# Two experts with 96 places share a group of 128 columns with two experts of 32 places: 25 groups instead of 26 in each mixture-of-experts layer

## The chip, the core and the metric

One core of a Trainium2 chip runs the whole kernel as one program. The metric is the device time of one execution in microseconds; all figures below are in us unless marked ns. The engines are called PE (TensorE, the matmuls), PEld (its weight loads), DVE (VectorE), ACT (ScalarE), POOL (GpSimd) and SP (SyncE, which issues the large DMAs).

## What is computed

A trunk of two layers over one sequence of 256 tokens with 1024 channels, all in fp32: a forgetting-attention layer and a native-sparse-attention layer, each followed by a mixture of experts. The mixture is what matters here:

```python
scores = jax.nn.sigmoid(h @ w_router)                 # 256 tokens x 64 experts
_, top_e = lax.top_k(scores + b_router, TOP_K)        # 8 experts of each token
top_s = jnp.take_along_axis(scores, top_e, axis=-1)
top_w = top_s / jnp.sum(top_s, axis=-1, keepdims=True) * ROUTED_SCALE
...
y = (jax.nn.silu(xb @ w_eg[e]) * (xb @ w_eu[e])) @ w_ed[e]     # 1024 -> 256 -> 1024
routed = segment_sum(y * row_w[:, None], row_tok, num_segments=T)
```

Every expert has 3 MB of weights (gate, up and down); 64 experts in each of two layers are 384 MB, which are read once.

## The kernel before, in words

**The ring of weights.** All large weights pass through `ring`, 14 slots of 1 MB. SP issues one DMA for each unit of 1 MB in the order of `ring_order` (L89): a unit may be issued once the unit 14 places before it has been used. For the experts, `used_by` (L1246) says what that is: the first halves of gate and up of a group are free at its semaphore `gu_half_out`, the second halves at `gu_out`, the down weights at the second `y_out`. An expert has three units, two of gate and up (`gate_up_unit`, L357) and one of down (`down_unit`, L360). After the last expert of the first layer the ring goes on with the units of the key/value projection, the adaLN vectors and the compression of the second layer.

**The groups.** PE works on experts in groups that together fill 128 columns, one column for each place, a place being one token of one expert. Experts 0 to 3 are static and take ranks 0 to 3; the other 60 are ranked at run time by how many tokens they have, most first. `expert_groups` (L63) fixes how many places a rank has: ranks 0 to 3 have 64 places and form two pairs, ranks 4 to 7 have 128 each and are alone (`LONE`), ranks 8 to 31 have 64 and form 12 pairs (`PAIRED`), ranks 32 to 63 have 32 and form 8 quads (`QUADS`). That makes 26 groups, in this order: two static pairs; four times a quad and a lone expert; four times three pairs and a quad. `GROUPS` is that list. If an expert has more tokens than places, a loop after the groups (`more_items`, L851) treats the rest in passes of 64 places. `capacity` (L1338, on POOL at the very start) holds the places of each rank, from which the number of such passes is worked out.

**A group on PE** (`pe_moe`, the loop at L951) is, in this order:
1. Gate and up, `pe_gate_up` (L817, matmul L823): for each of 8 blocks of 128 channels one matmul of 512 moving columns for each expert of the group, whose stationary operand is that expert's slice of the gathered tokens, 128, 64 or 32 columns wide. Each writes its own partitions of one PSUM bank. Four blocks come from the first half of the units, four from the second.
2. The gather of the next group's tokens, `pe_gather` (L813), by a one-hot matrix that DVE has made (`hot`, L1085): 16 matmuls.
3. Two transposes of the weighted one-hot matrix (L839) and two of the hidden rows (L841).
4. The combine of the group before, `pe_combine` (L846): 4 matmuls of 512 columns.
5. Down, `pe_down` (L831): 2 halves of 512 channels times 2 blocks of 128 hidden columns, for each expert one matmul of 512 columns.

Each fp32 matmul of the code is two load-and-matmul instructions in the trace, so a block of a lone expert shows x2, of a pair x4, of a quad x8.

ACT works on the silu (L1038), the copies of the gathered tokens (L1030) and of the transposes (L1043); DVE on the product (L1147), the one-hot matrices (L1087, L1095) and the scaling of the output (L1154). The instructions of one group are spread so that PE has work between the two halves of each of these chains. In the last group there is no gather, so step 5 comes sooner.

Of the kernel before, what the change touches and what calls it, by code (L numbers as in the profile page):

```python
# [24 lines left out]
ALU = mybir.AluOpType  # L25
# [3 lines left out]
P = 128  # L29
D = 1024  # L30
SEQ = 256
NT = SEQ // P
KC = D // P
# [18 lines left out]
PASS = 64  # L52
# [2 lines left out]


STATIC = 4
LONE = range(STATIC, 8)
PAIRED = range(8, 32)
QUADS = range(32, 64)  # L60


def expert_groups():  # L63

    lone = [[r] for r in LONE]
    pairs = [[r, r + 1] for r in PAIRED[::2]]
    quads = [list(range(r, r + 4)) for r in QUADS[::4]]
    out = [[0, 1], [2, 3]]
    for i in range(4):
        out += [quads[i], lone[i]]  # L70
    for i in range(4):
        out += pairs[3 * i:3 * i + 3] + [quads[4 + i]]
    return out


GROUPS = expert_groups()


# [68 lines left out]
def build(nc, a, out):  # L147
    with ExitStack() as ctx:
# [11 lines left out]
        PS = ctx.enter_context(nc.psum_tensor("PS", [P, 8, 512], F32))  # L160
        ring = sb("ring", [P, SLOTS, UNIT])
# [15 lines left out]
        iota = sb("iota", [P, IOTA])  # L177
# [24 lines left out]
        slot_ranked, weight_ranked = ranked[:, 0], ranked[:, 1]  # L202
        capacity = sb("capacity", [N_EXP, 1])
# [77 lines left out]
        x_more = cut(4864, [KC, PASS])  # L281
# [93 lines left out]
        group_sem = {n: sem(n) for n in PER_GROUP}  # L375
# [412 lines left out]
        GATHER, GU, Y0 = 4, 5, 6  # L788
# [69 lines left out]
        def pe_moe(pe_, layer):  # L858
            m = moe_sem[layer]
# [63 lines left out]
            for kind in range(2):  # L923
                for t in range(NT):
                    c = (kind * NT + t) * N_EXP
# [23 lines left out]
                return mm  # L949

            for g, group in enumerate(GROUPS):  # L951
                w = P // len(group)
                last = g == len(GROUPS) - 1
                pe_.wait_ge(*by_group("x_ready", layer, 2 * g + 2))
                for half in range(2):
                    for i in range(len(group)):
                        landed(pe_, gate_up_unit(layer, g, i, half))
                    slots = [slot_no(gate_up_unit(layer, g, i, half)) for i in range(len(group))]
                    pe_gate_up(pe_, slots, x_pair[g % 2], w, half
                               ).then_inc(group_sem["gu_out" if half else "gu_half_out"], 1)  # L960
                if g == 0:
                    item_ends()
# [22 lines left out]
                    landed(pe_, down_unit(layer, g, i))  # L985
                downs = [slot_no(down_unit(layer, g, i)) for i in range(len(group))]
                for half in range(2):
                    pe_down(pe_, downs, hidT[g % 2], w, half).then_inc(group_sem["y_out"], 1)
            combine(len(GROUPS) - 1).then_inc(unit_done, 3 * N_EXP)

            def one_more(i):
                pe_.wait_ge(*of_item(m, "onehot", i))
                pe_gather(pe_, hot_more, range(KC)).then_inc(m["more_products"], 1)
                pe_.wait_ge(*of_item(m, "x", i))
                pe_.wait_ge(m["more_loaded"], i * 48 + 48)
                pe_gate_up(pe_, [0], x_more, PASS, 0)
                pe_gate_up(pe_, [1], x_more, PASS, 1).then_inc(m["more_products"], 1)
# [4 lines left out]
                pe_down(pe_, [2], hidT[0], PASS, 0)  # L1002
                pe_down(pe_, [2], hidT[0], PASS, 1).then_inc(m["more_products"], 1)
# [53 lines left out]
        def dve_moe(done, layer):  # L1057
# [24 lines left out]
            def group_shape(x, n):  # L1082
                return x.to_broadcast([P, NT, n, P // n])

            def hot(g, slots):  # L1085
                n = len(GROUPS[g])
                return dve.tensor_tensor(one_hot[g % 2].rearrange("p t (n s) -> p t n s", n=n),  # L1087
                                         group_shape(iota[:, 1:1 + P // n].unsqueeze(1).unsqueeze(1), n),
                                         group_shape(slots[:, :, GROUPS[g][0]:GROUPS[g][0] + n].unsqueeze(3), n),
                                         ALU.is_equal)  # L1090

            def hot_weighted(g):
                n = len(GROUPS[g])
                r = GROUPS[g][0]
                return dve.tensor_tensor(hot_w.rearrange("p t (n s) -> p t n s", n=n),  # L1095
                                         one_hot[g % 2].rearrange("p t (n s) -> p t n s", n=n),
                                         group_shape(weight_ranked[:, :, r:r + n].unsqueeze(3), n), ALU.mult)
# [167 lines left out]
        def _(pool):  # L1265
# [67 lines left out]
            for e in range(STATIC):  # L1333
# [1 line left out]
                                        base=-e, pattern=[[1, N_EXP]], channel_multiplier=0))  # L1335
                done(pool.affine_select(out=key_col[:, :], in_=key_col[:, :], compare_op=ALU.not_equal, fill=FRONT * (STATIC - e),
                                        base=-e, pattern=[[0, 1]], channel_multiplier=1))
            done(pool.memset(capacity[:, :], float(P)))  # L1338
            for base, sign, slots in ((LONE.stop - 1, -1, 64), (-LONE.start, 1, 64), (QUADS.start - 1, -1, 32)):
                done(pool.affine_select(out=capacity[:, :], in_=capacity[:, :], compare_op=ALU.is_ge, fill=float(slots),  # L1340
                                        base=base, pattern=[[0, 1]], channel_multiplier=sign))
# [658 lines left out]
```

## Time and profile before

| | us |
|---|---|
| median of 3 runs | 1584.86 (1583.45 to 1586.05) |
| the profiled execution, its own time | 1586.27 |
| its span, first to last instruction | 1584.4 |
| PE busy | 1480.9 (93% of the span) |
| experts of layer 0, first gate/up to last combine | 304 to 776 |
| experts of layer 1 | 1106 to 1578 |

The profile comes from one execution. A timeline row gives the start, the duration, the engine, the line and the operation, then `out<-in`, the stationary shape (`128*32` is 128 rows by 32 columns) with the moving shape, and how many instructions the row merges. `[0.81 <-issue]` is the engine's idle time before it; "issue" is time in which the engine waited for nothing that the profile shows. For a DMA the answer on its line gives the number of issues, and the time from the issue to the landing. A stretch's row gives the busy time of each engine in it, the TensorE clock that was granted as a share of full speed, the mean busy share of the 16 DMA engines and what they moved in GB/s.

### The profile page before, as it was taken

To read this page: it belongs to the slowest core of one execution; us is meant where nothing else is said; L and a number is where in the kernel's file an instruction comes from. 1 tells how busy PE (TensorE), PEld (TensorE's weight loads), DVE (VectorE), ACT (ScalarE), POOL (GpSimd) and SP (SyncE) were. 2 spreads that over 40 slices of the span, in tenths; PEclk is the share of its full clock that TensorE was granted. 3 is DMA by queue.
4 is the path that set the end of the run, shared out by engine and by line. 5 is a ranking of instruction groups with operands and counts; after the bars stand their busy time and mean duration, and the time that the engine had idled before them with its cause. 6 is when DMAs were issued, how large, how long until landed. Compare 5 with 4: busy or idle time off the path is not lost.

```text
span 1584.4 us, 21198 instructions
## 1 busy us (share of the span) xinstructions
PE 1480.9 (93%) x8561; PEld 888.8 (56%) x8561; DVE 417.6 (26%) x969; ACT 280.8 (18%) x549; POOL 31.4 (2%) x81
## 2 busy tenths in 40 slices
PE   4999988999999999999798868789999999999998
PEld 2777777644555444454376757676455454544443
DVE  0466432111111111111367247522111111111111
ACT  2211332111111111111212215421111111111110
POOL 4000001000000000000000000001000000000000
PEclk9999987999999999999999768889999999999999
DMA  9967602399999999999999810031999999999996
GB/s 342 413 265 309 255 27 87 135 376 422 421 421 422 374 421 420 421 420 422 417 404 384 360 53 1 1 113 34 368 421 422 421 420 375 422 420 421 420 421 264
DMA packets 71315, 512.38 MB, mean 323 GB/s; under 512 B 8176, under 2 KB 8400, under 8 KB 9264
## 3 DMA queue, kind: packets, MB, share of 16 engines
q1 hardware_dynamic: 69984, 508.59, 78.5%
q0 software_dynamic: 800, 1.28, 0.4%
q8 instruction: 69, 1.13, 0.3%
q10 hardware_dynamic: 432, 1.13, 0.2%
q14 instruction: 30, 0.25, 0.0%
HBM read 509.92 MB, written 1.05 MB: 322 GB/s over the span
## 4 chain that ended last, share of the span: by engine, by line
PE 87%; DVE 5%; ACT 3%; issue 2%; DMA 1%; DVEq 0%; ACTq 0%
PE PS L823 23%; PE PS L446 13%; PE PS L813 12%; PE PS L831 12%; PE PS L846 11%; PE PS L875 2%; PE PS L616 2%; PE PS L404 2%; PE PS L469 2%; PE PS L483 1%; DMA h<-in_x 1%; PE PS L913 1%; PE PS L867 1%; DVE acc L527 1%; PE PS L586 1%
## 5 line engine op out<-in xcount | busy, mean ns | idle before, releaser
L823 PE MATMUL PS<-ring,scratch 128*32 128x512 f32 (+2 forms) x2048 | 367.8, 594 | 1.4 <-ACT scratch L1030 1.4
L823 PEld LDWEIGHTS PS<-ring,scratch 128*32 128x32 f32 (+2 forms) x2048 | 118.8, 127 | 243.7 <-issue 241.9
L446 PE MATMUL PS<-ring,uT 128*128 128x256 f32 x960 | 224.3, 395 | 2.9 <-ACT uT L417 1.8
L813 PEld LDWEIGHTS PS<-scratch,u 128*128 128x128 f32 x1664 | 190.8, 192 | 39.5 <-issue 37.6
L446 PEld LDWEIGHTS PS<-ring,uT 128*128 128x128 f32 x960 | 189.2, 199 | 31.8 <-ACT uT L417 2.6
L813 PE MATMUL PS<-scratch,u 128*128 128x128 f32 x1664 | 199.6, 278 | 1.4 <-ACT scratch L1030 1.4
L1154 DVE TENSOR_TENSOR scratch<-PS,gate_row 128x512 f32<-128x512 f32 x104 | 72.0, 692 | 464.1 <-PE PS L831 464.1
L831 PE MATMUL PS<-ring,scratch 128*32 128x512 f32 (+2 forms) x1024 | 189.3, 596 | 1.2 <-DVE item_first_i L1139 1.2
L846 PE MATMUL PS<-scratch 128*128 128x512 f32 x416 | 187.3, 593 | 0.0
L1038 ACT ACTIVATE scratch<-PS 128x256 f32<-128x256 f32 x52 | 20.0, 384 | 675.7 <-PE PS L823 675.7
L831 PEld LDWEIGHTS PS<-ring,scratch 128*32 128x32 f32 (+2 forms) x1024 | 56.8, 126 | 125.5 <-issue 123.8
L846 PEld LDWEIGHTS PS<-scratch 128*128 128x128 f32 x416 | 75.0, 190 | 76.3 <-issue 74.6
L1147 DVE TENSOR_TENSOR scratch<-scratch,PS 128x256 f32<-128x256 f32 x52 | 21.9, 422 | 337.5 <-ACT scratch L1038 337.5
L1030 ACT ACTIVATE scratch<-PS 128x512 f32<-128x512 f32 x104 | 62.1, 597 | 162.9 <-PE PS L813 162.9
L527 DVE SCALAR_TENSOR_TENSOR acc<-ring,cond,acc 128x256 f32<-128x256 f32 x168 | 81.5, 485 | 6.0
L483 PE MATMUL PS<-ring,scratch 128*32 128x256 f32 x512 | 42.5, 460 | 12.2 <-DVE scratch L1687 6.8
L616 PE MATMUL PS<-scratch,uT 128*128 128x65 f32 x288 | 38.4, 284 | 12.2 <-ACT uT L639 12.2
L616 PEld LDWEIGHTS PS<-scratch,uT 128*128 128x128 f32 x288 | 35.0, 196 | 19.3 <-ACT uT L639 17.3
L404 PE MATMUL PS<-ident,u 128*128 128x128 f32 x112 | 25.2, 419 | 18.4 <-ACT u L721 16.1
L647 ACT ACTIVATE scratch<-scratch,stats 128x128 f32<-128x128 f32 (+1 forms) x96 | 35.7, 443 | 19.0 <-DVE stats L666 19.0
L469 PE MATMUL PS<-four_rows,acc 128*128 128x1 f32 x128 | 22.8, 283 | 15.1 <-ACT acc L497 14.8
L404 PEld LDWEIGHTS PS<-ident,u 128*128 128x128 f32 x112 | 22.9, 227 | 20.4 <-issue 17.7
(306 smaller groups left out, 918.6 us busy)
## 6 DMA issues: line engine op xcount, KB each, us to landing
ring<-in_w_exp SPq DMA_DIRECT2D x384, 1024.0 KB, 15.5
ring<-in_w_ada_units SPq DMA_DIRECT2D x56, 1024.0 KB, 11.7
ring<-in_w_in_a_units SPq DMA_DIRECT2D x12, 1024.0 KB, 8.5
ring<-in_w_cmp_units SPq DMA_DIRECT2D x8, 1024.0 KB, 9.4
ring<-in_w_sh_units SPq DMA_DIRECT2D x6, 1024.0 KB, 16.2
ring<-in_w_kv_b_units SPq DMA_DIRECT2D x6, 1024.0 KB, 19.6
ring<-in_w_o_a_units SPq DMA_DIRECT2D x4, 1024.0 KB, 7.2
ring<-in_w_in_b_units SPq DMA_DIRECT2D x4, 1024.0 KB, 17.1
```

Source lines behind the costliest of these rows:

```text
L404: mm = pe_.transpose(PS[:, b, (k % 2) * SEQ + t * P:(k % 2) * SEQ + (t + 1) * P], src[:, t, k * P:(k + 1) * P], ident[:, :])
L446: mm = pe_.matmul(PS[:, bank, t * UC:(t + 1) * UC], lhs[:, k, t * P:(t + 1) * P], w[:, k, :], start=(k == 0), stop=(k == KC - 1))
L469: return [pe_.matmul(PS[:, ADA_COLUMNS, c0 + c:c0 + c + 1], part[:, c * P:(c + 1) * P], rows, start=True, stop=True) for c in range(2)]
L483: mm = pe_.matmul(PS[i:i + 32, ada_parts_bank(j), 0:UC], cond_cols[:, k, :], w[:, k, :], start=(k < 4), stop=(k >= 4))
L527: done(dve.scalar_tensor_tensor(out=sums, in0=w[:, k, :], scalar=cond[:, k:k + 1], in1=sums, op0=ALU.mult, op1=ALU.add), ada_products_read ...
L616: mm = pe_.matmul(PS[:, 6 + b % 2, hd * (DH + 1):(hd + 1) * (DH + 1)], pT[:, n * P:(n + 1) * P], values(br, kt, 4 * g + hd), start=(kt == ...
L813: mm = pe_.matmul(PS[:, bank, i * w:(i + 1) * w], u[:, t, k * P:(k + 1) * P], hot[:, t, :], start=(t == 0), stop=(t == NT - 1))
L823: mm = pe_.matmul(PS[i * w:(i + 1) * w, GU, :], x[:, kk, i * w:(i + 1) * w], gate_and_up, start=(kk == 0), stop=(kk == KC - 1))
L831: mm = pe_.matmul(PS[i * w:(i + 1) * w, Y0 + half, :], hT[:, j, i * w:(i + 1) * w], down[:, j, half * 512:(half + 1) * 512], start=(j == 0 ...
L846: mm = pe_.matmul(OUT[t][:, half * 512:(half + 1) * 512], hot_wT[0:rows, t * P:(t + 1) * P], y_rows[0:rows, half * 512:(half + 1) * 512], ...
L1030: act.activation(x_pair[g % 2][:, 4 * half:4 * half + 4, :].rearrange("p k s -> p (k s)"), PS[:, gather_bank(g, half), :], ACT.Copy).then_ ...
L1154: dve.tensor_tensor(y_rows[:, half * 512:(half + 1) * 512], PS[:, Y0 + half, :], gate_row[:, half * 512:(half + 1) * 512], ALU.mult).then_ ...
```

## The change

Ranks 4 and 5 stay alone with 128 places. Ranks 6 and 7 (`MIXED`) get 96 places instead of 128, and ranks 30 and 31 (`BESIDE_MIXED`) get 32 instead of 64. Ranks 6 and 30 form one group, 7 and 31 another; they stand where ranks 6 and 7 stood alone, as groups 7 and 9 counted from 0. The pair 30, 31, which was group 24, is gone. Every expert still has its three units; the six units of ranks 30 and 31 move from group 24 forward into groups 7 and 9. The new `column_tiles` cuts 96 places into a tile of 64 columns and one of 32, so a mixed group has three matmuls for each block: 64, 32 and 32 columns. DVE makes the one-hot matrix of a mixed group in two instructions instead of one, and its weighted form too.

```diff
-LONE = range(STATIC, 8)
-PAIRED = range(8, 32)
+LONE = range(STATIC, 6)
+MIXED = range(6, 8)
+PAIRED = range(8, 30)
+BESIDE_MIXED = range(30, 32)
 QUADS = range(32, 64)
+def slots_of(r):
+    return 128 if r in LONE else 96 if r in MIXED else 64 if r < BESIDE_MIXED.start else 32
 def expert_groups():
-    lone = [[r] for r in LONE]
+    lone = [[r] for r in LONE] + [[r, s] for r, s in zip(MIXED, BESIDE_MIXED)]
+def column_tiles(group):
+    tiles, at = [], 0
+    for i, r in enumerate(group):
+        left = slots_of(r)
+        while left:
+            n = 64 if left == 96 else left
+            tiles.append((i, slice(at, at + n)))
+            at, left = at + n, left - n
+    assert at == P
+    return tiles
...
-        def pe_gate_up(pe_, slots, x, w, half):
+        def pe_gate_up(pe_, slots, x, tiles, half):
             for k in range(KC // 2):
-                for i, s0 in enumerate(slots):
-                    gate_and_up = ring[:, s0, :].rearrange("p (k c) -> p k c", k=KC // 2)[:, k, :]
+                for i, places in tiles:
+                    gate_and_up = ring[:, slots[i], :].rearrange("p (k c) -> p k c", k=KC // 2)[:, k, :]
                     kk = half * KC // 2 + k
-                    mm = pe_.matmul(PS[i * w:(i + 1) * w, GU, :], x[:, kk, i * w:(i + 1) * w], gate_and_up,
+                    mm = pe_.matmul(PS[places, GU, :], x[:, kk, places], gate_and_up,
                                     start=(kk == 0), stop=(kk == KC - 1))
...
-        def pe_down(pe_, slots, hT, w, half):
+        def pe_down(pe_, slots, hT, tiles, half):
             for j in range(2):
-                for i, s0 in enumerate(slots):
-                    down = ring[:, s0, :].rearrange("p (j c) -> p j c", j=2)
-                    mm = pe_.matmul(PS[i * w:(i + 1) * w, Y0 + half, :], hT[:, j, i * w:(i + 1) * w],
+                for i, places in tiles:
+                    down = ring[:, slots[i], :].rearrange("p (j c) -> p j c", j=2)
+                    mm = pe_.matmul(PS[places, Y0 + half, :], hT[:, j, places],
                                     down[:, j, half * 512:(half + 1) * 512],
...
+            def runs(g):
+                ranks = GROUPS[g]
+                if len({slots_of(r) for r in ranks}) == 1:
+                    return [(ranks[0], len(ranks), 0, P // len(ranks))]
+                widths = [slots_of(r) for r in ranks]
+                return [(r, 1, sum(widths[:i]), widths[i]) for i, r in enumerate(ranks)]
             def hot(g, slots):
-                return dve.tensor_tensor(one_hot[g % 2].rearrange("p t (n s) -> p t n s", n=n),
                                         group_shape(iota[:, 1:1 + P // n].unsqueeze(1).unsqueeze(1), n),
                                         group_shape(slots[:, :, GROUPS[g][0]:GROUPS[g][0] + n].unsqueeze(3), n),
                                         ALU.is_equal)
+                for r, n, at, w in runs(g):
+                    ins = dve.tensor_tensor(places(one_hot[g % 2], n, at, w),
                                            iota[:, 1:1 + w].unsqueeze(1).unsqueeze(1).to_broadcast([P, NT, n, w]),
                                            slots[:, :, r:r + n].unsqueeze(3).to_broadcast([P, NT, n, w]), ALU.is_equal)
+                return ins
...
-            done(pool.memset(capacity[:, :], float(P)))
-            for base, sign, slots in ((LONE.stop - 1, -1, 64), (-LONE.start, 1, 64), (QUADS.start - 1, -1, 32)):
+            done(pool.memset(capacity[:, :], float(slots_of(0))))
+            for ranks in (LONE, MIXED, PAIRED, BESIDE_MIXED):
```

## Rows read from the trace of the kernel before

**Rows 1.** The page, in 40 slices of the span: mean busy tenths of the DMA engines.

```profile
DMA  9967602399999999999999810031999999999996
```

**Rows 2.** Stretches of both expert stages: us, each engine's busy time, PEclk, DMA share, GB/s.

```profile
520.00:540.00 20.00, 20.00 (x110) 9.21 (x110) 3.49 (x7) 2.07 (x4) 0.00 (x0) 1.00 0.86 336
540.00:560.00 20.00, 20.00 (x146) 9.06 (x140) 2.47 (x5) 2.07 (x4) 0.00 (x0) 1.00 0.99 415
740.00:760.00 20.00, 20.00 (x120) 9.14 (x120) 2.14 (x4) 2.07 (x4) 0.00 (x0) 1.00 1.01 420
1320.00:1340.00 20.00, 20.00 (x104) 9.44 (x102) 3.16 (x6) 2.07 (x4) 0.00 (x0) 1.00 0.94 380
1340.00:1360.00 20.00, 20.00 (x150) 8.85 (x148) 3.44 (x7) 2.07 (x4) 0.00 (x0) 1.00 0.92 372
```

**Rows 3.** The timeline of PE: a lone expert, a quad, two pairs, the last downs.

```profile
429.74 7.13 PE L823 MATMUL PS<-ring,scratch 128*128 128x512 f32 x16
447.68 7.07 PE L823 MATMUL PS<-ring,scratch 128*32 128x512 f32 x64
...
719.90 7.04 PE L823 MATMUL PS<-ring,scratch 128*64 128x512 f32 x32
...
734.51 3.65 PE L831 MATMUL PS<-ring,scratch 128*64 128x512 f32 x16
738.00 7.04 PE L823 MATMUL PS<-ring,scratch 128*64 128x512 f32 x32
...
768.37 3.64 PE L831 MATMUL PS<-ring,scratch 128*32 128x512 f32 x32
...
1570.79 3.64 PE L831 MATMUL PS<-ring,scratch 128*32 128x512 f32 x32
```

**Rows 4.** Waits of the DMA queue over the whole span: total, times, longest.

```profile
SPq L1215 <- PE PS L831: 432.1, 48, 10.4
```

**Rows 5.** Line 1215: last unit of each layer, then the 90 units up to the first.

```profile
L1215 SPq DMA_DIRECT2D ring<-in_w_exp x1: 332/332/332, 745.7 to 745.7; - x1
DMA to landing us min/median/max: 21.7/21.7/21.7
L1215 SPq DMA_DIRECT2D ring<-in_w_exp x1: 653/653/653, 1548.1 to 1548.1; - x1
DMA to landing us min/median/max: 21.5/21.5/21.5
L1215 SPq DMA_DIRECT2D ring<-in_w_exp x90: 332/333/1834, 538.5 to 745.7; - x90
DMA to landing us min/median/max: 5.0/17.7/28.1
```

**Rows 6.** The timeline of weight loads where the stationary width changes.

```profile
334.68 0.19 PEld L846 LDWEIGHTS PS<-scratch 128*128 128x128 f32 x1 [0.24 <-issue]
335.62 0.20 PEld L831 LDWEIGHTS PS<-ring,scratch 128*64 128x64 f32 x4 [0.76 <-issue]
336.11 0.14 PEld L831 LDWEIGHTS PS<-ring,scratch 128*64 128x64 f32 x2 [0.29 <-issue]
336.54 0.14 PEld L831 LDWEIGHTS PS<-ring,scratch 128*64 128x64 f32 x2 [0.28 <-issue]
...
338.25 0.14 PEld L831 LDWEIGHTS PS<-ring,scratch 128*64 128x64 f32 x2 [0.29 <-issue]
339.21 0.16 PEld L823 LDWEIGHTS PS<-ring,scratch 128*32 128x32 f32 x8 [0.81 <-issue]
339.67 0.13 PEld L823 LDWEIGHTS PS<-ring,scratch 128*32 128x32 f32 x4 [0.30 <-issue]
```

**Rows 7.** Between the layers: one adaLN unit's landing, and when DVE reads it.

```profile
L1195 SPq DMA_DIRECT2D ring<-in_w_ada_units x1: 328/328/328, 851.7 to 851.7; - x1
DMA to landing us min/median/max: 10.6/10.6/10.6
...
864.78 0.35 DVE L525 TENSOR_SCALAR acc<-ring,cond 128x256 f32<-128x256 f32 x1
```

More of the change, by code:

```diff
@@ L951, in pe_moe @@
             for g, group in enumerate(GROUPS):
-                w = P // len(group)
+                tiles = column_tiles(group)
                 last = g == len(GROUPS) - 1
@@ L958, in pe_moe @@
                     slots = [slot_no(gate_up_unit(layer, g, i, half)) for i in range(len(group))]
-                    pe_gate_up(pe_, slots, x_pair[g % 2], w, half
+                    pe_gate_up(pe_, slots, x_pair[g % 2], tiles, half
                                ).then_inc(group_sem["gu_out" if half else "gu_half_out"], 1)
@@ L987, in pe_moe @@
                 for half in range(2):
-                    pe_down(pe_, downs, hidT[g % 2], w, half).then_inc(group_sem["y_out"], 1)
+                    pe_down(pe_, downs, hidT[g % 2], tiles, half).then_inc(group_sem["y_out"], 1)
             combine(len(GROUPS) - 1).then_inc(unit_done, 3 * N_EXP)
@@ L995, in one_more @@
                 pe_.wait_ge(m["more_loaded"], i * 48 + 48)
-                pe_gate_up(pe_, [0], x_more, PASS, 0)
-                pe_gate_up(pe_, [1], x_more, PASS, 1).then_inc(m["more_products"], 1)
+                pe_gate_up(pe_, [0], x_more, [(0, slice(0, PASS))], 0)
+                pe_gate_up(pe_, [1], x_more, [(0, slice(0, PASS))], 1).then_inc(m["more_products"], 1)
                 pe_.wait_ge(*of_item(m, "hid", i))
@@ L1001, in one_more @@
                 pe_.wait_ge(*of_item(m, "copied", i))
-                pe_down(pe_, [2], hidT[0], PASS, 0)
-                pe_down(pe_, [2], hidT[0], PASS, 1).then_inc(m["more_products"], 1)
+                pe_down(pe_, [2], hidT[0], [(0, slice(0, PASS))], 0)
+                pe_down(pe_, [2], hidT[0], [(0, slice(0, PASS))], 1).then_inc(m["more_products"], 1)
                 pe_.wait_ge(*of_item(m, "y", i))
@@ L1080, in dve_moe, with places @@
                                           op0=ALU.add, op1=ALU.mult), routing["unranked_ready"])
-            def group_shape(x, n):
-                return x.to_broadcast([P, NT, n, P // n])
-            def hot(g, slots):
-                n = len(GROUPS[g])
-                return dve.tensor_tensor(one_hot[g % 2].rearrange("p t (n s) -> p t n s", n=n),
-                                         group_shape(iota[:, 1:1 + P // n].unsqueeze(1).unsqueeze(1), n),
-                                         group_shape(slots[:, :, GROUPS[g][0]:GROUPS[g][0] + n].unsqueeze(3), n),
-                                         ALU.is_equal)
-            def hot_weighted(g):
[L1093 to L1097, printed above, removed]
+            def runs(g):
[4 more added lines that the diff above has]
+                return [(r, 1, sum(widths[:i]), widths[i]) for i, r in enumerate(ranks)]
+            def places(x, n, at, w):
+                return x[:, :, at:at + n * w].rearrange("p t (n s) -> p t n s", n=n)
+            def hot(g, slots):
+                for r, n, at, w in runs(g):
+                    ins = dve.tensor_tensor(places(one_hot[g % 2], n, at, w),
+                                            iota[:, 1:1 + w].unsqueeze(1).unsqueeze(1).to_broadcast([P, NT, n, w]),
+                                            slots[:, :, r:r + n].unsqueeze(3).to_broadcast([P, NT, n, w]), ALU.is_equal)
+                return ins
+            def hot_weighted(g):
+                for r, n, at, w in runs(g):
+                    ins = dve.tensor_tensor(places(hot_w, n, at, w), places(one_hot[g % 2], n, at, w),
+                                            weight_ranked[:, :, r:r + n].unsqueeze(3).to_broadcast([P, NT, n, w]), ALU.mult)
+                return ins
             done(hot(0, unranked[:, 0]), group_sem["onehot_ready"])
@@ L1337, in _ @@
                                         base=-e, pattern=[[0, 1]], channel_multiplier=1))
-            done(pool.memset(capacity[:, :], float(P)))
-            for base, sign, slots in ((LONE.stop - 1, -1, 64), (-LONE.start, 1, 64), (QUADS.start - 1, -1, 32)):
-                done(pool.affine_select(out=capacity[:, :], in_=capacity[:, :], compare_op=ALU.is_ge, fill=float(slots),
-                                        base=base, pattern=[[0, 1]], channel_multiplier=sign))
+            done(pool.memset(capacity[:, :], float(slots_of(0))))
+            for ranks in (LONE, MIXED, PAIRED, BESIDE_MIXED):
+                done(pool.affine_select(out=capacity[:, :], in_=capacity[:, :], compare_op=ALU.is_ge,
+                                        fill=float(slots_of(ranks.start)), base=ranks.start - 1, pattern=[[0, 1]],
+                                        channel_multiplier=-1))
             done(pool.iota(iota[:, :], pattern=[[1, IOTA]], base=0, channel_multiplier=0,
```

## The prediction

> **What bounds the kernel now.** I read four views in this order. First the page's slices: over both expert stages the DMA engines are busy in nine tenths or more of nearly every slice [rows 1]. Then stretches of 20 us: PE is busy 20.00 of 20 at full clock, and in the same stretch the DMA engines stand at 1.01 with 420 GB/s; there are only two places in a stage where the DMA falls behind that, 336 and 415 GB/s in layer 0, 380 and 372 in layer 1 [rows 2]. So both are full, and it must be found out which one gives the end. The waits say that SP waits for PE to free ring slots, 432 us in 48 waits on the down matmuls [rows 4]: PE sets the pace, and DMAs queue behind it. But the lead is nearly spent at the end of a stage. The last unit of layer 0 is issued at 745.7 and lands 21.7 later, at 767.4, and the matmuls that need it start at 768.37; in layer 1 it lands at 1548.1 + 21.5 = 1569.6 and is used at 1570.79 [rows 5, 3]. The slack is 0.97 and 1.19 us. Anything that makes PE faster by more than about 1 us meets the DMA, and anything that makes the DMA later by more than that is paid in full.
>
> **What goes.** One group of each layer. From pair to pair it is 738.00 - 719.90 = 18.10 us [rows 3]. A lone expert, a pair and a quad have gate/up of 7.13, 7.04 and 7.07 us [rows 3], so a group costs the same whatever it holds, and its place is dear. PE alone would gain 18.1 us per layer. The bytes stay: 192 units per layer, no DMA goes.
>
> **What comes: the mixed groups.** In a block of a pair or a quad all tiles run beside each other: one block is 7.04 / 8, with the last matmul's tail off about 0.86 us, for two beats of 0.43 (336.11 to 336.54) [rows 3, 6]. A mixed group has tiles of 64, 32 and 32 columns in every block, so the width changes twice per block. What a change of width costs is seen where one operation follows another. From 64 to 32 columns the last loads before are at 338.25, their matmuls' successors would load at 338.68, and the 32-wide loads come at 339.21, with 0.81 us idle before them where 0.29 is usual. From 128 to 64 columns it is the same: 334.68, then 335.62, 0.76 idle [rows 6]. The loads, which are else a beat ahead, wait until the matmuls of the other width are through, 0.53 us after the last of them has started. Then the two beats of the new width are 0.46 apart (339.21 to 339.67) at 32 columns and 0.49 (335.62 to 336.11) at 64 [rows 6]. If that holds within a block too, the 64-wide tile takes 0.49 + 0.53 = 1.02 us, the two 32-wide ones together 0.46 + 0.53 = 0.99, and a block 2.0 us instead of 0.86: 1.14 more. Gate/up has 8 blocks, down 4: 12 x 1.14 = 13.7 us per mixed group, 27.4 per layer.
>
> No row shows two widths on disjoint columns: all changes in the trace are on overlapping ones. So this price lies between two ends. The lower is nothing, 0.86 per block, if the chip minds only overlap. The upper is all three tiles one after another, 1.02 + 2 x 0.99 = 3.0. I take 2.0, because both rows of a change show the same wait though the overlap differs (32 in 64, 64 in 128), and the quad's row shows that tiles of one width do run together.
>
> The Trainium skill, TensorEngine Tiling (Array Packing), Key Properties, says that changing the tiling mode, not merely the tile, drains TensorE; by it the block is 2.0 us and the time the forecast below. No run here shows it for disjoint tiles. The same list says that tiles are independent, which alone would give the first rival.
>
> **The sum for PE.** Per layer +27.4 - 18.1 = +9.3 us.
>
> **The sum for the DMA.** The ring has 14 slots, so a slow PE starves it of slots and that time is not made up. Today the last long stall ends when unit 102 of a layer's 192 gets its slot, freed by the first down of group 12 (unit 88): issued 538.5, landed 5.0 later at 543.5; that is the first of the 90 units up to the last [rows 5]. From there 89 landings take 767.4 - 543.5 = 223.9, or 2.52 each. After the change group 12 ends 27.4 later (both mixed groups lie before it) and frees the slot of unit 108, since 6 units have moved ahead of it; 83 landings remain. The last landing moves by 27.4 - 6 x 2.52 = +12.3. Less the slack it is +11.3 in layer 0 and +11.1 in layer 1. That is more than PE's own 9.3, so the DMA gives the end and PE waits some 2 us before the last down.
>
> **Does layer 0's part reach the end?** Between the layers PE and DVE work through units that landed earlier. The shortest lead that I find is a unit issued at 851.7 that lands at 862.3 and is read by DVE at 864.78, 2.5 us [rows 7]. PE's end moves by 11.3 and the stream of landings by 12.3, so 1 us of that lead goes and the whole shift is carried on.
>
> **Small parts, at nothing.** Four more DVE instructions per layer for one-hot matrices: DVE is busy 2 to 3.5 of 20 us [rows 2] and makes them a group ahead; with its cover gone each is under half a microsecond. One more affine select on POOL at the start, hundreds of us before its first reader. SP reads one more rank per mixed group, while it waits for slots anyway [rows 4]. Widths change once more before and after a mixed group, about 0.1 us each, in the rounding.
>
> **Forecast.** 11.3 + 11.1 = +22.4 us. The profiled execution took 1586.27, which would become 1608.7; it stands 1.4 above the median of 1584.86, so for the median I say 1607.
>
> **Rivals.**
> (a) *Disjoint tiles of unlike width run together.* A block stays at 0.86, PE would gain 18.1 per layer, and then it meets the DMA. Slack of 0.97 and 1.19 goes first. Beyond that only the DMA's own idle time can be won: against 421 GB/s, 336 and 415 in 20 us each are 4.0 + 0.3 us in layer 0, 380 and 372 are 1.9 + 2.3 in layer 1 [rows 2]. Six units instead of three in groups 7 and 9 keep the ring hungry and would close these gaps. Sum 4.3 + 0.97 + 4.2 + 1.19 = 10.7, time 1574. It decides below the point where the DMA's last landing doesn't move beyond its slack: 27.4 replaced by 15.1 + 1.0, a block of about 1.53 us. For it: quads show four tiles at once, on disjoint columns. Against it: the loads' wait at each change of width [rows 6].
> (b) *Nothing is shared in a mixed group*, the two 32-wide tiles wait for each other too. A block is 3.0, 12 x 2.14 = 25.7 per group, 51.4 per layer; less 15.1 and the slack, 35 per layer, time 1655. Against it: the two are of one width, as in a quad.
> (c) *Cancelled out.* The drain is half hidden, a block is near 1.5 and gain and loss meet within 0.2%, 3.2 us. Nothing in the rows gives such a value; it needs an accident.
> (d) *Too few places.* The reference's routing gives the ranks 6 and 7 77 and 71 tokens in layer 0 and 82 and 68 in layer 1, and the ranks 30 and 31 30 or 31 each, so all fit, by one place. If the core counted otherwise, a pass after the groups would come, at least a group's 18.1 us [rows 3] and three loads of 2.5 that nothing hides, some 26 us for each. Very unlikely.
>
> **Chances.** The drain, with a block between 1.72 (no beats shared, nothing lost at the change) and 2.2: 0.76. Rival (a) 0.17, (b) 0.04, (c) 0.02, (d) 0.01. A block of 1.72 gives 20.6 - 15.1 - 0.97 = 4.5 and 4.3, time 1594; PE's own +2.5 is less. A block of 2.2 gives 1617. To hold 8 in 10 the range must take (b) as well: 1594 to 1655. Faster by over 0.2% is (a) alone, 0.17; within 0.2% (about what a measurement of this kernel can tell from none) 0.02; slower 0.81.
>
> **What would show it.** In the timeline of a mixed group gate/up (L823 before) should take about 16 us instead of 7.1 and down about 8 instead of 3.6, with weight loads in twos and fours some 1.0 us apart, and idle time before each change. The mean busy share of PE in those stretches stays high, as the tails fill it. SP's waits for PE should grow, DMA slices should fall behind at groups 7 to 13, and PE should wait about 2 us for a landing before the last down. Under (a) gate/up would stay at 7, there would be no dip in GB/s, and PE would wait for landings in several groups. The forecast is wrong if a block takes less than 1.5 us, or if the stage's end moves by another amount than the last landing.

## The result, and the profile after

The changed kernel takes 1613.63 us (median of 4 runs, 1610.19 to 1614.28), the kernel before 1585.45 beside it (4 runs); the ratio is 1.0178 with a 95% interval of 1.0163 to 1.0193. It is slower, as forecast, by 28.2 us where 22.4 were forecast.

The profiled execution took 1613.28 us with a span of 1611.5. To see where the time went, both spans are cut at four starts that the timelines show: first gate/up and last down of each layer. The span of the kernel before was 1584.4 us, so the two lie 27.1 apart.

| part | before | after | difference | forecast |
|---|---|---|---|---|
| start to first gate/up of layer 0 | 304.1 | 303.1 | -1.0 | 0 |
| to its last down | 464.3 | 475.5 | +11.2 | +11.3 |
| to first gate/up of layer 1 | 338.1 | 343.8 | +5.7 | 0 |
| to its last down | 464.3 | 475.4 | +11.1 | +11.1 |
| to the end | 13.7 | 13.7 | 0.0 | 0 |

Both expert stages moved as the working said, to 0.2 us. The miss is in the part between them, whose work no line of the diff changes.

The timeline of PE of the changed kernel, for the first mixed group, the quad after it, and the last group of each layer (columns as in [rows 3]):

```profile
428.80 15.95 PE L843 MATMUL PS<-ring,scratch 128*64 128x512 f32 x48
444.68 3.84 PE L833 MATMUL PS<-scratch,u 128*128 128x128 f32 x32
...
452.32 7.58 PE L851 MATMUL PS<-ring,scratch 128*64 128x512 f32 x22
459.29 0.62 PE L843 MATMUL PS<-ring,scratch 128*32 128x512 f32 x2
459.73 0.60 PE L851 MATMUL PS<-ring,scratch 128*32 128x512 f32 x2
459.74 7.45 PE L843 MATMUL PS<-ring,scratch 128*32 128x512 f32 x62
...
764.05 3.64 PE L843 MATMUL PS<-ring,scratch 128*32 128x512 f32 x32
768.65 3.64 PE L843 MATMUL PS<-ring,scratch 128*32 128x512 f32 x32 [0.96 <-DMA ring<-in_w_exp]
...
778.59 3.64 PE L851 MATMUL PS<-ring,scratch 128*32 128x512 f32 x32 [1.13 <-DMA ring<-in_w_exp]
...
1597.80 3.64 PE L851 MATMUL PS<-ring,scratch 128*32 128x512 f32 x32 [1.08 <-DMA ring<-in_w_exp]
```

Gate/up of the group of ranks 6 and 30 takes 15.95 us where a lone expert had 7.13 [rows 3]. Down's row is 7.58 us long and ends where the next group's first tiles are mixed in; the other mixed group's down is one row of 8.01 us. In the last group PE now stands still twice for a landing, 0.96 us before the second half of gate/up and 1.13 before down; before there was no such wait and 0.97 us of slack [rows 3, 5].

The weight loads of the same mixed group, in twos for the 64-wide tile and in fours for the two 32-wide ones (columns as in [rows 6]):

```profile
428.79 0.19 PEld L843 LDWEIGHTS PS<-ring,scratch 128*64 128x64 f32 x2 [0.84 <-issue]
429.80 0.14 PEld L843 LDWEIGHTS PS<-ring,scratch 128*32 128x32 f32 x4 [0.81 <-issue]
430.78 0.19 PEld L843 LDWEIGHTS PS<-ring,scratch 128*64 128x64 f32 x2 [0.84 <-issue]
```

This is the forecast's mechanism seen directly. The two loads of the 64-wide tile come at 428.79, the four of the 32-wide tiles 1.01 us later, the next 64-wide ones 0.98 after that. A block is 1.99 us. The 32-wide tiles use other columns of the array than the 64-wide tile, and yet their loads come 0.81 us after the load engine fell idle, as they did in [rows 6] where the columns overlapped.

The stretches of layer 0 around and after the mixed groups, and one near its end (columns as in [rows 2]):

```profile
420.00:440.00 20.00, 20.00 (x91) 5.98 (x92) 1.78 (x4) 1.35 (x3) 0.00 (x0) 1.00 1.02 423
...
480.00:500.00 20.00, 20.00 (x84) 7.22 (x83) 0.76 (x2) 2.06 (x4) 0.00 (x0) 1.00 1.01 421
500.00:520.00 20.00, 20.00 (x89) 7.31 (x88) 2.47 (x5) 0.98 (x2) 0.00 (x0) 1.00 0.80 322
520.00:540.00 20.00, 20.00 (x105) 10.24 (x105) 2.47 (x5) 3.15 (x6) 0.00 (x0) 1.00 0.87 353
540.00:560.00 20.00, 20.00 (x98) 9.63 (x97) 2.47 (x5) 2.07 (x4) 0.00 (x0) 1.00 0.88 358
560.00:580.00 20.00, 20.00 (x138) 8.90 (x140) 2.47 (x5) 2.06 (x4) 0.00 (x0) 1.00 0.86 351
...
740.00:760.00 20.00, 20.00 (x98) 9.57 (x96) 2.14 (x4) 2.07 (x4) 0.00 (x0) 1.00 1.01 421
```

The kernel before has a count nearly as low in one stretch:

```profile
480.00:500.00 20.00, 20.00 (x94) 9.69 (x94) 2.47 (x5) 2.07 (x4) 0.00 (x0) 1.00 1.01 422
```

PE is at 20.00 throughout, and nothing in that column says that its work takes twice as long. The number of matmuls says it only faintly: x84 to x91 where mixed groups are, but x98 stands at 740 to 760 without one, and x94 in the row of the kernel before. The weight loads say it better. They are busy 6.0 to 7.3 us in the three stretches with mixed groups (420, 480 and 500) and 8.9 to 10.2 in the others shown. The DMA follows behind: 322, 353, 358 and 351 GB/s in four stretches in a row, against 421, where the same place in [rows 2] had 336 in one stretch and 415 in the next. The waits, of PE for a landing, over both layers:

```profile
PE PS L851 <- DMA ring<-in_w_exp: 2.2, 2, 1.1
PE PS L843 <- DMA ring<-in_w_exp: 1.9, 2, 1.0
```

and of SP's queue for slots:

```profile
SPq L1242 <- PE PS L851: 432.5, 46, 13.5
SPq L1242 <- PE PS L843: 208.9, 84, 6.9
```

where the kernel before had, for gate/up:

```profile
SPq L1215 <- PE PS L823: 186.3, 89, 3.1
```

SP's wait for the down matmuls is 432.5 us, as before [rows 4]: there are fewer such waits (46 against 48), and the longest is longer (13.5 us against 10.4). Its wait for gate/up has grown by 22.6 us, with one of 6.9 where 3.1 was the longest.

### The profile page after: what moved, and what is told of

It is laid out like the page before. It is cut to its first block, busy times and chain, and to the rows that moved or that the text cites. A ratio compares the mean times of both kernels' runs of the same rounds, so it can differ in the third digit from the quotient of the medians.

```text
span 1611.5 us, 21200 instructions
## 1 busy us (share of the span) xinstructions
PE 1504.2 (93%) x8569; PEld 875.0 (54%) x8569; DVE 413.3 (26%) x967; ACT 276.3 (17%) x541; POOL 31.4 (2%) x82
## 3 DMA queue, kind: packets, MB, share of 16 engines
q8 instruction: 69, 1.13, 0.3%
q10 hardware_dynamic: 432, 1.13, 0.2%
## 4 chain that ended last, share of the span: by engine, by line
PE 85%; DVE 5%; DMA 4%; ACT 3%; issue 2%; DVEq 0%; ACTq 0%; SPq 0%
PE PS L843 23%; PE PS L466 12%; PE PS L851 12%; PE PS L833 11%; PE PS L866 10%; DMA ring<-in_w_exp 3%; PE PS L636 2%; PE PS L895 2%; PE PS L424 2%; PE PS L489 1%; DVE acc L547 1%; PE PS L503 1%; DMA h<-in_x 1%; PE PS L623 1%; PE PS L933 1%
## 5 line engine op out<-in xcount | busy, mean ns | idle before, releaser
L843 PE MATMUL PS<-ring,scratch 128*32 128x512 f32 (+2 forms) x2112 | 391.0, 595 | 3.3 <-DMA ring<-in_w_exp 1.9
L843 PEld LDWEIGHTS PS<-ring,scratch 128*32 128x32 f32 (+2 forms) x2112 | 113.7, 123 | 272.6 <-issue 270.9
L466 PEld LDWEIGHTS PS<-ring,uT 128*128 128x128 f32 x960 | 188.2, 198 | 31.1 <-ACT uT L437 2.2
L833 PEld LDWEIGHTS PS<-scratch,u 128*128 128x128 f32 x1600 | 183.2, 192 | 39.3 <-issue 37.4
L851 PE MATMUL PS<-ring,scratch 128*32 128x512 f32 (+2 forms) x1056 | 199.7, 598 | 3.4 <-DMA ring<-in_w_exp 2.2
L833 PE MATMUL PS<-scratch,u 128*128 128x128 f32 x1600 | 192.4, 278 | 1.4 <-ACT scratch L1050 1.4
L866 PE MATMUL PS<-scratch 128*128 128x512 f32 x400 | 180.1, 593 | 0.0
L851 PEld LDWEIGHTS PS<-ring,scratch 128*32 128x32 f32 (+2 forms) x1056 | 54.4, 123 | 140.9 <-issue 139.3
L636 PE MATMUL PS<-scratch,uT 128*128 128x65 f32 x288 | 44.9, 315 | 10.7 <-ACT uT L659 10.6
L636 PEld LDWEIGHTS PS<-scratch,uT 128*128 128x128 f32 x288 | 41.3, 226 | 18.9 <-ACT uT L659 15.6
```

Of the source, the lines that this page charges most:

```text
L466: mm = pe_.matmul(PS[:, bank, t * UC:(t + 1) * UC], lhs[:, k, t * P:(t + 1) * P], w[:, k, :], start=(k == 0), stop=(k == KC - 1))
L636: mm = pe_.matmul(PS[:, 6 + b % 2, hd * (DH + 1):(hd + 1) * (DH + 1)], pT[:, n * P:(n + 1) * P], values(br, kt, 4 * g + hd), start=(kt == ...
L833: mm = pe_.matmul(PS[:, bank, i * w:(i + 1) * w], u[:, t, k * P:(k + 1) * P], hot[:, t, :], start=(t == 0), stop=(t == NT - 1))
L843: mm = pe_.matmul(PS[places, GU, :], x[:, kk, places], gate_and_up, start=(kk == 0), stop=(kk == KC - 1))
L851: mm = pe_.matmul(PS[places, Y0 + half, :], hT[:, j, places], down[:, j, half * 512:(half + 1) * 512], start=(j == 0), stop=(j == 1))
L866: mm = pe_.matmul(OUT[t][:, half * 512:(half + 1) * 512], hot_wT[0:rows, t * P:(t + 1) * P], y_rows[0:rows, half * 512:(half + 1) * 512], ...
```

## The experiments

**Equal tiles.** The changed kernel with one line changed: 96 places become three tiles of 32.

```diff
-            n = 64 if left == 96 else left
+            n = 32 if slots_of(r) == 96 else left
```

> The changed kernel with one edit: 96 places are cut into three tiles of 32 columns instead of one of 64 and one of 32, so a mixed group has four tiles of one width. Theory 1 (tiles of unlike width exclude each other, tiles of one width run together): gate/up of a mixed group takes 7.1 us and down 3.6 instead of 15.9 and 7.9; PE would then save 18.1 per layer and meet the DMA, so the expert stage (first gate/up to last down) goes from 464.3 before to about 458.5 to 460 and no further, PE waits for landings in several groups, and the time is 1572 to 1577, up to 4 us off by what the part between the layers does. Theory 2 (the price is that two experts of unlike size share a group, or that a mixed group has more matmuls per block): gate/up stays above 12 us and the time at 1600 or more. Theory 3 (PE alone gives the end): 36 us less than before, 1549.

It took 1577.76 us (6 runs, 1576.54 to 1579.46), ratio to the kernel before 0.9942 (0.9921 to 0.9963), so it beats both kernels. Its timeline around the first mixed group and in the last group of layer 0:

```profile
428.00 7.05 PE L843 MATMUL PS<-ring,scratch 128*32 128x512 f32 x64
...
442.62 3.64 PE L851 MATMUL PS<-ring,scratch 128*32 128x512 f32 x32
...
451.13 3.64 PE L843 MATMUL PS<-ring,scratch 128*32 128x512 f32 x32 [1.43 <-DMA ring<-in_w_exp]
...
745.26 3.64 PE L843 MATMUL PS<-ring,scratch 128*32 128x512 f32 x32
752.34 5.34 PE L843 MATMUL PS<-ring,scratch 128*32 128x512 f32 x32 [3.44 <-DMA ring<-in_w_exp]
...
762.79 3.64 PE L851 MATMUL PS<-ring,scratch 128*32 128x512 f32 x32
```

Gate/up of the mixed group is 7.05 us and down 3.64, with four matmuls per block. The number of tiles and the company of two experts cost nothing on PE; the unlike width is the whole loss. But the stage is 460.4 us (458.5 to 460 expected), only 4.0 shorter than before, for 18.1 us less work on PE. Most of the rest is in the waits, here over both layers:

```profile
PE PS L843 <- DMA ring<-in_w_exp: 20.3, 13, 3.4
```

PE waits 20.3 us for landings, 13 times, where the kernel before never did; 10.1 us of it are layer 0's. This is what rival (a) said of the DMA: PE gets faster and meets it. A further 1.7 us of layer 0 is the clock. After the wait of 3.44 us the second half of gate/up takes 5.34 us instead of 3.64, and the granted clock is 0.53 of full speed over the first two thirds of it, almost all at 1.2 GHz:

```profile
752.34:755.90 3.56, 3.56 (x20) 1.25 (x24) 0.00 (x0) 0.00 (x0) 0.00 (x0) 0.53 1.03 428
```

Layer 1's last group does the same, with 5.34 us after a wait of 3.19. The two stretches from 520 on where the DMA had fallen behind are full:

```profile
520.00:540.00 20.00, 20.00 (x104) 9.27 (x100) 3.16 (x6) 2.07 (x4) 0.00 (x0) 1.00 1.01 420
540.00:560.00 20.00, 20.00 (x150) 8.99 (x150) 3.50 (x7) 2.07 (x4) 0.00 (x0) 1.00 1.01 421
```

**Halving the changes of width.** The tiles stay 64, 32, 32; the loops are turned, so that each half does all its 64-wide matmuls first.

```diff
-            for k in range(KC // 2):
-                for i, places in tiles:
+            for wide in sorted({p.stop - p.start for _, p in tiles}, reverse=True):
+                for k in range(KC // 2):
+                    for i, places in [t for t in tiles if t[1].stop - t[1].start == wide]:
```

`pe_down` in the same way.

> The changed kernel with the tiles kept (64, 32, 32) but the loops turned: in each half, all 64-wide matmuls first and then all 32-wide ones, so that gate/up changes width 4 times instead of 16 and down 4 times instead of 8. Theory 1 (unlike widths exclude each other, and the change itself costs 0.1 us): the two widths still take turns, 2 x 0.86 us per block, so gate/up is about 14.2 us and down about 7.1; a mixed group costs 11 us more than a lone one instead of 13.4, the stage is about 470 to 471 against 475.5, the time about 1603. Theory 2 (only the change costs, about 0.57 us each, and tiles of unlike width overlap in between): gate/up 7 + 4 x 0.6 = 9.4, down about 6, and the time near or below the kernel before, 1585.

It took 1601.66 us (4 runs, 1600.29 to 1610.53), ratio 1.0106 (1.0067 to 1.0145). The stage is 471.3 us (470 to 471 expected), gate/up of the mixed group 14.34 (14.2 expected), by PE's timeline:

```profile
428.13 14.34 PE L844 MATMUL PS<-ring,scratch 128*64 128x512 f32 x48
```

Its weight loads, around the change from the 64-wide matmuls of a half to the 32-wide ones, and back:

```profile
430.75 0.14 PEld L844 LDWEIGHTS PS<-ring,scratch 128*64 128x64 f32 x1 [0.29 <-issue]
431.70 0.14 PEld L844 LDWEIGHTS PS<-ring,scratch 128*32 128x32 f32 x4 [0.81 <-issue]
432.16 0.12 PEld L844 LDWEIGHTS PS<-ring,scratch 128*32 128x32 f32 x2 [0.31 <-issue]
432.59 0.12 PEld L844 LDWEIGHTS PS<-ring,scratch 128*32 128x32 f32 x2 [0.31 <-issue]
...
434.31 0.12 PEld L844 LDWEIGHTS PS<-ring,scratch 128*32 128x32 f32 x2 [0.31 <-issue]
435.26 0.19 PEld L844 LDWEIGHTS PS<-ring,scratch 128*64 128x64 f32 x2 [0.84 <-issue]
```

Within one width a load comes every 0.43 to 0.46 us, alone or in twos; at the change 0.95 pass instead. A lone 64-wide stream occupies the array for as long as a full one does, while half of its columns stand idle. So the 13.4 us that a mixed group costs more are mostly that two widths take turns (in this version gate/up takes 14.34 - 7.13 = 7.2 us more than a lone expert's), and only the rest is the change itself: 12 fewer changes in gate/up (4 instead of 16) save 15.95 - 14.34 = 1.6 us, 0.13 each.

**The cut without the merge.** The 26 groups of before, but the lone experts of rank 6 and 7 in tiles of 64, 32 and 32. The ranges of ranks are those of before again; the other edit is in `column_tiles`:

```diff
+    if group in ([6], [7]):
+        return [(0, slice(0, 64)), (0, slice(64, 96)), (0, slice(96, 128))]
```

> The groups of the kernel before (26, nothing merged), but the 128 columns of the experts of rank 6 and 7 are cut into tiles of 64, 32 and 32. Same expert, same units, same places: only the cut of the matmuls is new. Theory 1 (the cut alone is the loss): gate/up of these two groups 15.9 and down 7.9 us, 13.4 us more each; PE and the last landing both move by 26.8 per layer, so the stage goes from 464.3 to 491, and the time to 1585 + 54 = 1639, up to 6 us off by the part between the layers. Theory 2 (sharing a group is what costs): no change, 1585.

It took 1646.26 us (2 runs), ratio 1.0371 (1.0332 to 1.0409); 1633 to 1645 was expected, and the excess is in the part between the layers (345.2 us, below). The two stages are 491.2 us each, 26.9 more than before, and gate/up shows the same 15.95:

```profile
429.44 15.95 PE L845 MATMUL PS<-ring,scratch 128*64 128x512 f32 x48
```

The cut costs 26.9 us a layer, and merging gives back 15.8 us (491.2 to 475.5), not the 18.1 of a group: the other 2.3 are lost to landings, as the next run shows.

**Who gives the end of the stage.** Layer 1 of two kernels with DMAs of half a unit: the changed kernel from group 14 on, and the one with equal tiles from group 4 on. The other half of the columns keeps older weights, so the output of layer 1's experts is not the reference's; all matmuls are done.

```diff
-                    sp.dma_start(ring[:, slot_no(n):slot_no(n) + 1, :], src).then_inc(slot_loaded[slot_no(n)], 16)
+                    half_only = layer == 1 and at + SLOTS >= GROUP_AT[14]
+                    cols = slice(0, UNIT // 2 if half_only else UNIT)
+                    sp.dma_start(ring[:, slot_no(n):slot_no(n) + 1, cols], src[:, :, cols]).then_inc(slot_loaded[slot_no(n)], 16)
```

> The changed kernel; in layer 1, from group 14 on, each DMA of a weight unit brings only the first half of its columns (the rest of the slot keeps older weights), so PE, DVE and ACT do the same work and landings come sooner. Layer 0 is untouched. Theory 1 (in the changed kernel the starved ring and not PE gives the end, by some 2 us per layer): layer 1's stage falls from 475.4 to what PE alone needs, 464.33 - 18.1 + 26.8 = 473.1 us. Theory 2 (PE gives the end): 475.4 as in layer 0, which stays at 475.5 in either case.

> The version with three tiles of 32 columns, with halved DMAs in layer 1 from group 4 on; layer 0 untouched. Theory 1 (with equal tiles only the DMA keeps the gain of 18.1 us from coming through): layer 1's stage is 464.33 - 18.1 = 446.2 us, against 460.4 in layer 0. Theory 2 (something else on PE, DVE or ACT takes the rest of the gain): well above 447, up to 460.

The changed kernel's layer 1 takes 473.1 us against 475.4 for layer 0 in the same execution. The last group has lost both waits:

```profile
1581.04 7.07 PE L843 MATMUL PS<-ring,scratch 128*32 128x512 f32 x64
...
1593.23 3.64 PE L851 MATMUL PS<-ring,scratch 128*32 128x512 f32 x32
```

So in the changed kernel 2.3 us of a stage are the DMA's. With equal tiles layer 1 takes 446.4 us against 460.1 in layer 0: PE's gain of 18.1 us is there to 0.2 us. What held it back are the landings, and the low clock that followed the longest wait for one: with light DMAs neither is there. Both runs were single ones.

**PE off the path altogether.** Equal tiles, and the combine of every group but the last left out.

```diff
-                    combine(g - 1)
+                    pe_.wait_ge(*by_group("y_ready", layer, 2 * g))
```

> The version with three tiles of 32 columns, and the combine matmuls of every group but the last left out (so only the last group's rows reach the output of the experts). That takes 24 x 3.5 = 84 us per layer off PE and not one byte off the DMA. Theory 1 (with equal tiles the DMA gives the end of the expert stage): the stage goes from 460.4 to 455 to 460 us, since only the stalls of the DMA at its start can shrink; PE then waits 80 us or so for landings. Theory 2 (PE still gives the end): the stage falls to about 376 us.

This is a single run. Layer 0's stage is 457.5 us, 2.9 shorter for 84 us less of PE, so the DMA and not PE gives the end with equal tiles. Its waits up to there:

```profile
PE PS L843 <- DMA ring<-in_w_exp: 55.0, 22, 6.3
PE PS L851 <- ACT scratch L1063: 18.0, 23, 0.8
PE PS L851 <- DMA ring<-in_w_exp: 1.7, 1, 1.7
```

PE waits 56.7 us for landings, not 80. Part of the 84 goes to another wait, 18.0 us for ACT's copy of the transposes: the combine had been its cover. The clock takes another part. By its records it is at 1.2 GHz for 38.2 us of this stage, which is worth about 19 us of full clock; in the kernel before and in the changed one it is at 2.4 GHz in the whole stage. Layer 1 of this run says nothing on the stage, since its input was changed. Two passes follow its groups, so more tokens than places must have fallen to some expert. They give the price that rival (d) only bounded. Gate/up of the two passes:

```profile
1579.02 8.66 PE L843 MATMUL PS<-ring,scratch 128*64 128x512 f32 x16 [8.33 <-DMA ring<-in_w_exp]
...
1610.08 8.49 PE L843 MATMUL PS<-ring,scratch 128*64 128x512 f32 x16 [7.71 <-DMA ring<-in_w_exp]
```

From one to the next it is 31.1 us, 7.7 of them waiting for the pass's own weights (8.3 in the first); the estimate was 26.

**The part between the layers.** It grew by 5.7 us, though its work is the same. Two kernels delay the end of layer 0 and change nothing else. They are the kernel before, with the first half of the last gather done three or six times more.

```diff
+                    if layer == 0 and g == 24:
+                        for _ in range(3):
+                            pe_gather(pe_, one_hot[(g + 1) % 2], range(0, 4))
```

> The kernel before, groups and tiles untouched; in layer 0, ahead of the last group's gather, the first half of that gather is done three times more with the same result, which delays PE by 3 x 1.9 = 5.7 us and nothing else. Layer 0's stage grows from 464.3 to 470.0. The question is the part between the layers (last down of layer 0 to first gate/up of layer 1), 338.1 us before and 343.8 after the change. Theory 1 (its length depends on when the granted clock of TensorE falls to half in it, which shifts with the time at which the stage ends): it need not stay at 338.1, and whatever it becomes is 338.1 + 0.42 x (time at half clock in it - 99.0), to 0.5 us. Theory 2 (the change itself makes it longer, by the later weights or the other groups): it stays at 338.1 to 338.5, and so does its time at half clock.

> The same with six repeats, 11.4 us: about the shift that the change gives at this place. Layer 0's stage is 475.7. Theory 1: as for three repeats, the length follows the time at half clock with 0.42 us for each us, and at least one of the two delays gives more than 339.5. Theory 2: 338.1 to 338.5 in both.

They took 1591.87 and 1605.64 us (one run each). Layer 0's stage came out at 469.7 and 475.1 us, where 470.0 and 475.7 were expected.

And the changed kernel was run again:

> The changed kernel once more. The expert stages are set by work counts and landings and come out at 475.4 to 475.5 each. Theory 1 (clock): the part between the layers may differ from 343.8, by the same line 338.1 + 0.42 x (time at half clock - 99.0), which is what spreads its runs over 1610 to 1614. Theory 2 (the change lengthens it): 343.8 again.

It took 1610.35 us (2 runs), ratio 1.0156 (1.0126 to 1.0185), and its stages 475.7 and 475.2 us.

Here is the part between the layers of five executions, each from its last down of layer 0 to its first gate/up of layer 1 (columns as in [rows 2]): the kernel before,

```profile
768.37:1106.46 338.09, 288.00 (x1738) 228.29 (x1737) 166.74 (x411) 97.56 (x198) 6.74 (x5) 0.85 0.47 187
```

the changed kernel,

```profile
778.59:1122.35 343.76, 294.36 (x1738) 233.99 (x1738) 166.74 (x411) 97.33 (x198) 6.72 (x5) 0.84 0.47 185
```

the changed kernel again,

```profile
779.24:1119.56 340.32, 290.47 (x1738) 230.22 (x1738) 166.75 (x411) 97.49 (x198) 6.74 (x5) 0.85 0.47 186
```

the delay of three,

```profile
772.86:1112.07 339.21, 288.79 (x1738) 228.93 (x1737) 166.66 (x411) 97.39 (x198) 6.74 (x5) 0.85 0.46 179
```

and of six:

```profile
778.39:1125.93 347.54, 296.47 (x1738) 237.38 (x1737) 166.75 (x411) 97.73 (x198) 6.74 (x5) 0.83 0.44 173
```

PE has 1738 matmuls in each and DVE 166.66 to 166.75 us; but PE's busy time goes from 288.00 to 296.47 and its granted clock from 0.85 to 0.83. What is left beside PE's busy time is 49.4 to 51.1 us, so the growth is in the matmuls themselves and not in waits. The level is 1.2 GHz in part of this stretch and 2.4 in the rest. The clock records, summed over it, give:

| kernel | time at half clock | length |
|---|---|---|
| before | 99.0 | 338.1 |
| equal tiles | 99.0 | 338.5 |
| delay of three | 99.0 | 339.2 |
| changed, again | 102.4 | 340.3 |
| turned loops | 105.8 | 341.1 |
| changed | 112.6 | 343.8 |
| lone experts cut | 116.1 | 345.2 |
| delay of six | 119.5 | 347.5 |

The expectation's line, 338.1 + 0.42 x (half clock - 99.0), was drawn through the five profiles there were then (before, equal tiles, turned loops, changed, lone experts cut). The two delays and the changed kernel run again lie above it by 1.1, 0.8 and 0.8 us, outside the 0.5 that was set. So do the three runs with light DMAs or without the combine: 338.8, 340.4 and 341.3 us with 99.0, 102.4 and 105.1 at half clock, 0.6 to 0.9 above. The order holds and the size nearly does. The question between the two theories is settled all the same. The kernel before, only delayed, has the longest part of all, 347.5 us, and the changed kernel has had 343.8, 340.3 and, in layer 0 of its run with light DMAs, 340.4. So neither the other groups nor the later weights are needed to lengthen it; it goes with the time at the low clock. An example is the first projection unit after layer 0. In the kernel before it ran at full clock:

```profile
786.52 7.14 PE L446 MATMUL PS<-ring,uT 128*128 128x256 f32 x32 [1.14 <-ACT uT L426]
```

and in the changed one partly at half:

```profile
797.13 9.02 PE L466 MATMUL PS<-ring,uT 128*128 128x256 f32 x32 [1.14 <-ACT uT L446]
```

In both, PE waits 6.5 us for ACT before the transposes ahead of this unit, and in both the clock falls. In the kernel before it does so 9.6 us after the last down's start and is back before the unit begins:

```profile
778.00:784.80 6.80, 2.68 (x13) 2.71 (x14) 2.71 (x6) 4.43 (x8) 1.48 (x2) 0.50 1.02 408
```

In the changed kernel it falls 12.1 us after the last down's start, and stays down longer and into the unit:

```profile
790.70:800.90 10.20, 7.42 (x25) 6.36 (x26) 6.53 (x18) 3.19 (x5) 0.46 (x1) 0.50 1.01 408
```

Why it fell earlier and for less time in one of them is left open.

## Why the prediction was right, and where it was not

- *A place of a group costs 18.1 us whatever it holds.* Right: with equal tiles and light DMAs the stage is shorter by 464.33 - 446.38 = 17.95.
- *A block of unlike widths takes 2.0 us.* Right, 1.99; 13.7 us per mixed group were 13.4 and 13.5. What the rows of before could not show, that disjoint columns don't help, the changed kernel shows. The Trainium skill's rule (TensorEngine Tiling (Array Packing), Key Properties) is that changing the tiling mode drains TensorE. The trace agrees, by the loads at 429.80 and 430.78 with 0.81 and 0.84 us of idle time before them. Its other rule in that list is that tiles operate independently. The runs bear it out among tiles of one width only: gate/up is 7.05 us with four tiles of 32 and 15.95 with 64, 32 and 32.
- *The starved ring gives the end.* Right: +12.3 for the last landing less the slack gave +11.3 and +11.1, measured +11.2 and +11.1. The last landing itself moved by 12.0 and 12.1, counted from the first gate/up. With light DMAs 2.3 us go and 8.8 are left, which is PE's own part, 9.3 in the forecast. Two details were wrong. The wait is split, half of it before the second half of gate/up of the last quad, not all before down. And SP's waits for PE grew on gate/up, by 22.6 us, and not on down.
- *The whole shift is carried on between the layers.* This step failed. It looked for a lead of the landings that might break, found 2.5 us, and took the length of the part for fixed. It is fixed in its work and not in its clock: 338.1 to 347.5 us over eleven executions. The span of the profiled execution is 27.1 us longer than that of the kernel before, 4.7 more than the 22.4 of the sum: this part gave 5.7 and the start took 1.0 back. In the second profiled execution of the same kernel it gave 2.2. All six runs of the changed kernel (1610.1 to 1614.3) are above the 1607 that was said, so the term that was put at nothing is not noise around zero here. What the runs show is its range, 0 to 9.4 us, and that it goes with the time at 1.2 GHz; what places that time stays open. That the total came within 7 us of 1607 all the same is in part luck: nothing in the forecast said that this term would be small.
- *Small parts at nothing.* Nothing contradicts it: the stages of the turned loops, the cut and the light runs come out at counts of PE's work and landings alone, to about 0.3 us.
- *Rival (a)*, tested by equal tiles: 1577.8 where 1574 was worked out. The mechanism was right, but the stage gave 4.0 us and not 5.3. Two terms were too large. The last landing came 3.7 us sooner after the first gate/up, where 4.3 of idle DMA were to be won. And of the slack of 0.97 only 0.3 was used: the down matmuls start at 762.79, 0.6 us after the last landing at 762.15. What they wait for is the chain behind the wait of 3.44 us, 10.45 us from 752.34 to 762.79, which the low clock made 1.7 us longer. The prediction had no clock in this sum. It also said that the DMA falls behind at only two places of a stage; the stretches 320 to 340 and 340 to 360 have 352 and 401 GB/s in layer 0 of the kernel before, and with equal tiles the first of them still has 330.
- *Rival (b)*, a block of 3.0, is out by the row of loads in fours.

## What to carry to other kernels

Cut the columns of concurrent matmuls into tiles of one width, also where a wider tile would save an instruction: here 64 beside 32 took turns even on disjoint columns, and a 64-wide tile alone held the array as long as four tiles of 32. Before paying for less PE work, read how far the landings are ahead at the end of the stage and how much idle time the DMA has; here 1 us of lead and some 4 us of idle DMA meant that 18.1 us less of matmuls returned 4.0. A busy share of 20.00 in 20 tells neither of the two; the busy time of the weight loads and the GB/s beside it do.

## What the runs showed of the hardware that was not expected

- The part between the layers differs by up to 9.4 us between executions with the same work, by how long the granted clock is at 1.2 GHz in it; a difference of a few us in the time of such a kernel can be that alone. Cutting the span at fixed events separates it: five expert stages of the changed kernel took 475.2 to 475.7 us.
- Faster work can bring the low clock with it. With equal tiles PE stood still for 3.44 us at the end of a stage and then ran the next matmuls at 1.2 GHz, 1.7 us lost; without the combine, with PE idle for 77 us of the stage, 38.2 us of it were at 1.2 GHz.
- The rows at 459.29 and 459.73 show matmuls out of the order of the program: two 32-wide ones of the quad's gate/up start before the last two of the mixed group's down, which stand ahead of them. They have the same width and other columns. So a matmul on free columns can pass earlier ones of its own width; in the rows shown none passes one of another width.
